# The last expert pair loaded in column halves, and the token tiles finished in another order

## The reference, cut to what matters

```python
def moe(h, ...):            # 4 groups, top-1; then top-2 of the group's 8 experts
    ...
    hg = jnp.einsum('nd,edf->nef', x, w_gate)
    hu = jnp.einsum('nd,edf->nef', x, w_up)
    act = jax.nn.silu(hg) * hu * combine[:, :, None]
    return jnp.einsum('nef,efd->nd', act, w_down)

x = x + g1 * mixers(x)      # called x1 below
x = x + g2 * moe(h2, ...)   # the outputs y_sample (4 tiles) and y_prompt (1 tile)
```

## Time and profile before

| | |
|---|---|
| median of three runs | 633.35 us |
| the profiled execution | 631.55 us, its span 629.6 us |
| TensorE, VectorE, ScalarE, GpSimd busy | 94%, 56%, 28%, 15% |
| granted TensorE clock, mean | 0.992 |
| bytes moved | 176.23 MB, mean 280 GB/s |
| chain that ended last | TensorE 67%, DMA 15%, SyncE's queue 7%, VectorE 6% |

### The profile page before, as it was taken

How to read it: one execution, slowest core, us unless ns; L and a number is a source line. 1 busy time by engine, 2 the same in 40 slices (tenths; PEclk the granted TensorE clock), 3 DMA queues, 4 the chain that set the end, 5 groups by cost and what they waited for, 6 DMA issues and landing times.

```text
span 629.6 us, 9459 instructions
## 1 busy us (share of the span) xinstructions
PE 593.3 (94%) x3309; PEld 331.4 (53%) x3310; DVE 352.3 (56%) x788; ACT 177.5 (28%) x369; POOL 94.6 (15%) x131
## 2 busy tenths in 40 slices
PE   4989999999998999999999889999999999689797
PEld 2544555555565676645555445555555555355453
DVE  2736898765664888655666873343424334313337
ACT  4203887601144787731111101101110110011110
POOL 4000011122161000000000111212122121201200
PEclk9999999999999999999999999999999999989999
DMA  8999843330029629529114959999999999999876
GB/s 318 375 370 361 318 156 138 140 133 2 0 83 280 249 92 264 238 102 398 67 68 161 382 188 392 417 419 416 420 420 410 420 417 421 419 421 416 360 280 263
DMA packets 48273, 176.23 MB, mean 280 GB/s; under 512 B 10988, under 2 KB 18168, under 8 KB 34544
## 3 DMA queue, kind: packets, MB, share of 16 engines
q1 hardware_dynamic: 36992, 154.86, 63.0%
q0 software_dynamic: 6688, 15.58, 7.1%
q10 hardware_dynamic: 4560, 5.35, 2.4%
HBM read 163.31 MB, written 21.14 MB: 293 GB/s over the span
## 4 chain that ended last, share of the span: by engine, by line
PE 67%; DMA 15%; SPq 7%; DVE 6%; issue 2%; ACT 1%; ACTq 1%; POOL 1%; DVEq 0%; POOLq 0%
PE ps L1757 16%; PE ps L1574 11%; PE ps L1773 7%; PE ps L1490 7%; PE ps L1502 6%; DMA expert_w<-exp_w_up 5%; PE ps L1612 4%; PE ps L1639 4%; DMA gate_w<-lru_wx 3%; PE ps L1621 3%; DMA w_mod_ring<-w_mod 2%; SPq L329 2%; SPq L358 2%; PE ps L1465 2%; PE ps L1725 2%
## 5 line engine op out<-in xcount | busy, mean ns | idle before, releaser
L1757 PE MATMUL ps<-expert_w,hT_mixT 128*64 128x256 f32 x1120 | 137.1, 395 | 11.9 <-DMA expert_w<-exp_w_up 11.6
L1757 PEld LDWEIGHTS ps<-expert_w,hT_mixT 128*64 128x64 f32 x1120 | 84.8, 137 | 67.6 <-issue 23.0
L1490 PE MATMUL ps<-hT_mixT,w 128*128 128x128 f32 (+1 forms) x256 | 72.6, 437 | 1.2 <-DVE hT_mixT L918 1.2
L1574 PE MATMUL ps<-w,hT_mixT 128*128 128x512 f32 x160 | 71.9, 597 | 0.0
L1773 PE MATMUL ps<-expert_w,w 128*64 128x512 f32 x280 | 65.8, 598 | 0.0
L741 ACT ACTIVATE w<-ps 128x128 f32<-128x128 f32 x36 | 10.0, 278 | 194.4 <-PE ps L1757 194.4
L1304 DVE SCALAR_TENSOR_TENSOR w<-w,ps 128x128 f32<-128x128 f32 x36 | 10.4, 288 | 88.0 <-ACT w L741 88.0
L1490 PEld LDWEIGHTS ps<-hT_mixT,w 128*128 128x128 f32 x256 | 38.9, 191 | 35.8 <-issue 32.6
L1502 PE MATMUL ps<-w_qkv,hT_mixT 128*128 128x512 f32 (+1 forms) x160 | 53.2, 488 | 0.2 <-DVE v_tok L1006 0.2
L1322 DVE TENSOR_TENSOR w<-ps,w 128x1024 f32<-128x1024 f32 x17 | 20.8, 1225 | 56.5 <-PE ps L1773 56.5
L1574 PEld LDWEIGHTS ps<-w,hT_mixT 128*128 128x128 f32 x160 | 29.1, 191 | 29.9 <-issue 29.7
(11 more groups left out here) (289 smaller groups left out, 763.6 us busy)
## 6 DMA issues: line engine op xcount, KB each, us to landing
expert_w<-exp_w_down SPq DMA_DIRECT2D x31, 1024.0 KB, 18.5
expert_w<-exp_w_gate SPq DMA_DIRECT2D x29, 1024.0 KB
expert_w<-exp_w_up SPq DMA_DIRECT2D x29, 1024.0 KB
w_mod_ring<-w_mod SPq DMA_DIRECT2D x14, 1024.0 KB, 6.5
y_rows<-zero_rows POOLq DMA_DIRECT2D x10, 512.0 KB, 9.4
expert_w<-y_rows SPq DMA_DIRECT2D x10, 512.0 KB, 8.3
recurrence<-w_mod SPq DMA_DIRECT2D x8, 512.0 KB, 9.7
w<-w_in SPq DMA_DIRECT2D x4, 1024.0 KB, 16.9
```

Of the source, the lines that this page charges most:

```text
L1490: ins = pe.matmul(ps[:, bank, 0:n], w1v[:, c, m * P:(m + 1) * P], HM[:, c, lo:lo + n], start=(c == 0), stop=(c == DC - 1))
L1574: ins = pe.matmul(ps[:, 2 * (t % 2) + half, :], HM[:, c, t * P:(t + 1) * P], w1v[:, c, half * 512:(half + 1) * 512], start=(c == 0), stop= ...
L1757: ins = pe.matmul(ps[r, 2 + k, 0:2 * P].rearrange("p (k f) -> p k f", k=2), xT[:, c, r], gate_up(i)[:, :, c, k:FF:FC], start=(c == 0), sto ...
```

## The change

Four things are changed together.

- Pair 15 is loaded by `refill_for_halves`: when the place's gate and up sums are done, eight DMAs of 512 KB (first column half of gate and up of both experts, then the second) in place of four of 1 MB. TensorE's last step waits for the first half (`halves_in`, 128), does 32 matmuls, waits for the second (`wgu_in`), does the others.
- The tiles are finished in the order 3, 4, 0, 1, 2, and `PE_SUMS` is 4, 0, 1. The y rows are read in that order.
- The three x1 reads are issued behind the y reads of tiles 3 and 4, whose x1 is in SBUF; `with_second` waits for them for tiles 0, 1 and 2 alone.
- On VectorE `with_second(3)` stands before the eviction of the last step's rows.

```diff
-PE_SUMS = (1, 2, 3)
+ORDER = (3, 4, 0, 1, 2)
+PE_SUMS = (4, 0, 1)
...
+            def refill_for_halves(q, s):
+
+                done = sp.value_load(last[0:1, q - HELD:q - HELD + 1])
+                sp.wait_ge(S["gu_mm"], done * FC)
+                for half in range(2):
+                    for j in range(2 * s, 2 * s + 2):
+                        for src, lo in ((wg_v, 0), (wu_v, EW)):
+                            sp.dma_start(ring[:, HOME[j], lo + half * EW // 2:lo + (half + 1) * EW // 2],
+                                         src[q * 2 + (j - 2 * s), :, half * EW // 2:(half + 1) * EW // 2])\
+                              .then_inc(wgu_in[s] if half else halves_in, 16)
+                sp.wait_ge(S["dn_mm"], done)
+                for j in range(2 * s, 2 * s + 2):
+                    w_down(sp, q * 2 + (j - 2 * s), j)
...
-            refill(PAIRS - 1, 0)
-            sp.wait_ge(kept_in, 16 * 4)
-            for t in range(SPILLED):
-                sp.dma_start(x1b[:, t, :], a["x1_rows"][t * P:(t + 1) * P, :]).then_inc(kept_in, 16)
+            refill_for_halves(PAIRS - 1, 0)
...
-            for t in range(NT):
+            sp.wait_ge(kept_in, 16 * 4)
+            for t in ORDER:
                 sp.dma_start(yk[:, t, :], ...).then_inc(rows_in[t], 16)
                 sp.dma_start(y0[:, t, :], ...).then_inc(y0_in[t], 16)
...
+                if t == ORDER[1]:
+                    for k in range(SPILLED):
+                        sp.dma_start(x1b[:, k, :], a["x1_rows"][k * P:(k + 1) * P, :]).then_inc(kept_in, 16)
...
             def with_second(t):
...
-                dve.wait_ge(kept_in, 16 * (4 + SPILLED))
+                if t < SPILLED:
+                    dve.wait_ge(kept_in, 16 * (4 + SPILLED))
...
+            with_second(3)
             last_y_evict(end)
+            with_first(3)
+            finish(0)
+            with_second(4)
             with_second(0)
-            with_first(0)
+            finish(1)
             with_second(1)
-            finish(0)
+            finish(2)
             with_second(2)
-            finish(1)
-            with_second(3)
-            with_second(4)
-            finish(2)
-            with_first(4)
+            with_first(2)
             finish(3)
             finish_last()
...
+                if by_halves:
+                    pe.wait_ge(halves_in, 128)
...
                 for half in range(2):
+                    if by_halves and half:
+                        pe.wait_ge(wgu_in[s], visit * 64)
```

More of the change, by code:

```diff
@@ L499, in _ @@
             sp.sem_inc(S["sp_turn"], 1)
-            for t in range(NT):
+            sp.wait_ge(kept_in, 16 * 4)
+            for t in ORDER:
                 sp.dma_start(yk[:, t, :], a["y_rows"][TOK + t * P:TOK + (t + 1) * P, :]).then_inc(rows_in[t], 16)
                 sp.dma_start(y0[:, t, :], a["y_rows"][t * P:(t + 1) * P, :]).then_inc(y0_in[t], 16)
-            for t in range(NT - 1):
-                sp.wait_ge(S["fin"], t + 1)
-                sp.dma_start(y_dst[t], yk[:, t, :]).then_inc(S["out_done"], 16)
+                if t == ORDER[1]:
+                    for k in range(SPILLED):
+                        sp.dma_start(x1b[:, k, :], a["x1_rows"][k * P:(k + 1) * P, :]).then_inc(kept_in, 16)
+            for i in range(NT - 1):
+                sp.wait_ge(S["fin"], i + 1)
+                sp.dma_start(y_dst[ORDER[i]], yk[:, ORDER[i], :]).then_inc(S["out_done"], 16)
             for half in range(2):
@@ L508, in _ @@
                 cols = slice(half * 512, (half + 1) * 512)
-                sp.dma_start(y_dst[NT - 1][:, cols], yk[:, NT - 1, cols]).then_inc(S["out_done"], 16)
+                sp.dma_start(y_dst[ORDER[-1]][:, cols], yk[:, ORDER[-1], cols]).then_inc(S["out_done"], 16)
             sp.wait_ge(S["out_done"], 16 * (NT + 2))
@@ L1343, in with_first, with finish @@
                 step(dve.tensor_tensor(yk[:, t, :], yk[:, t, :], y0[:, t, :], ALU.add))
-            def finish(t):
-                dve.wait_ge(S["tail_mm"], t + 1)
-                b = 2 * t % 8
+            def finish(i):
+                dve.wait_ge(S["tail_mm"], i + 1)
+                t, b = ORDER[i], 2 * i % 8
                 dve.tensor_tensor(yk[:, t, :], yk[:, t, :], wide[:, b * 512:b * 512 + D], ALU.add)\
@@ L1351, in finish_last @@
             def finish_last():
-                b = 2 * (NT - 1) % 8
+                t, b = ORDER[-1], 2 * (NT - 1) % 8
                 for half in range(2):
@@ L1356, in finish_last @@
                     cols = slice(half * 512, (half + 1) * 512)
-                    dve.tensor_tensor(yk[:, NT - 1, cols], yk[:, NT - 1, cols], ps[:, b + half, :], ALU.add)\
+                    dve.tensor_tensor(yk[:, t, cols], yk[:, t, cols], ps[:, b + half, :], ALU.add)\
                        .then_inc(S["fin"], 1)
@@ L1730, in act_in, with step_of @@
                 pe.transpose(ps[:, 4 + 3 * c, 0:P], act2[:, c, :], ident[:, :]).then_inc(S["aT_mm"], 1)
-            def step_of(n, s, visit, kept=False):
+            def step_of(n, s, visit, kept=False, by_halves=False):
                 def gate_up(i):
@@ L1747, in step_of @@
                     pe.wait_ge(kept_in, 16 * 4)
-                else:
+                elif not by_halves:
                     pe.wait_ge(wgu_in[s], visit * 64)
-                if s == 0 and not (isinstance(visit, int) and visit == 1):
+                if by_halves:
+                    pe.wait_ge(halves_in, 128)
+                elif s == 0 and not (isinstance(visit, int) and visit == 1):
                     pe.wait_ge(halves_in, 64)
                 for half in range(2):
+                    if by_halves and half:
+                        pe.wait_ge(wgu_in[s], visit * 64)
                     for k in range(FC):
@@ L1788, in _, with visits @@
             pe.wait_ge(S["route_ok"], 3)
-            def visits(q, s, visit, kept=False):
+            def visits(q, s, visit, kept=False, by_halves=False):
                 lo = pe.value_load(first[0:1, bass.ds(q, 1)])
@@ L1793, in visits @@
                 with pe.Fori(lo, hi) as n:
-                    step_of(n, s, visit, kept)
+                    step_of(n, s, visit, kept, by_halves)
             for s in range(HELD):
@@ L1800, in _ @@
             for q in range((BODIES - 1) * HELD, PAIRS):
-                visits(q, q % HELD, 1 + q // HELD, kept=q == KEPT // 2)
+                visits(q, q % HELD, 1 + q // HELD, kept=q == KEPT // 2, by_halves=q == PAIRS - 1)
             steps = pe.value_load(last[0:1, PAIRS - 1:PAIRS])
@@ L1806, in _ @@
             pe.wait_ge(S["xT_a"], steps + 1)
-            for t in range(NT):
-                if t >= 4:
-                    pe.wait_ge(S["fin"], t - 3)
+            for i, t in enumerate(ORDER):
+                if i >= 4:
+                    pe.wait_ge(S["fin"], i - 3)
                 if t in PE_SUMS:
@@ L1812, in _ @@
                 for half in range(2):
-                    if t == 0:
+                    if i == 0:
                         pe.wait_ge(S["y_v"], steps + 1 + half)
                     if t in PE_SUMS:
-                        pe.matmul(ps[:, 2 * t % 8 + half, :], ident[:, :], y0[:, t, half * 512:(half + 1) * 512],
+                        pe.matmul(ps[:, 2 * i % 8 + half, :], ident[:, :], y0[:, t, half * 512:(half + 1) * 512],
                                   start=True, stop=False)
-                    ins = pe.matmul(ps[:, 2 * t % 8 + half, :], chosen[:, t, :],
+                    ins = pe.matmul(ps[:, 2 * i % 8 + half, :], chosen[:, t, :],
                                     y[:, half * 512:(half + 1) * 512], start=t not in PE_SUMS, stop=True)
-                    if half or t == NT - 1:
+                    if half or i == NT - 1:
                         ins.then_inc(S["tail_mm"], 1)
```

## The result

The changed kernel takes 634.42 us (median of 20 runs, 632.44 to 637.9); the kernel before, in 20 runs beside it, 632.32 (629.74 to 634.2). The ratio is 1.0034, 95% interval 1.0019 to 1.0048: 2.1 us slower, where I had forecast 0.6 faster. The profiled execution takes 632.74 us, 1.2 over that of before, with a span of 630.7. So one part of the loss stands in this trace and another, about 0.9 us, only in the median: the profiled execution is the third fastest of the 20.

The account below looks back on a forecast made before the run. The tail was taken to be VectorE's, with the reads a little ahead. VectorE ending 0.7 us earlier, plus 0.1 for TensorE's clock, gave -0.6 us: 632.7 from the median of 633.35, range 629.5 to 634.9.

Parts of the forecast that it names:

- TensorE's earlier start: Last step's gate and up sums: start at 593.0, not 596.24, take 7.47 us and end 4.9 us earlier.
- Down weights just in time: Last step's down sums, due at 601.7: their two down transfers land at 601.0 or a little over.
- The scatter: Last scatter, from 595.41: ends at 602.3 without x1 rows on its rings; first y read at 602.4 instead of 603.09.
- First read: First y read of the tail: lands 3.4 us after issue, at 605.8, where it took 4.2 us before.
- The wait of VectorE before `with_second(0)`: VectorE in the tail: idles 3 us for the x1 reads and tile 0's y row, landing at 615.2.
- Rival D: Pair 15's loads: each half-size transfer pays 2.9 us by itself on the slowest ring, end +5 us, 638.4; chance 0.03.
- Its four matmuls for a tile take 1.72 us (the pitch from 618.28 to 620.00): TensorE in the tail: a tile's sums take 1.72 us, 3.4 at half clock, tile 0's sum then at 619.9.
- 605.8 + 12 x 1.34 = 621.9: Tail reads: thirteen at 1.34 us each after the first; the last lands 2.5 us later than the tenth did.
- I count 0.1: TensorE's idling before tile 0's first row lowers its clock: 0.1 us added to the end.
- Rival A: Tail reads cost more than they free: scatter ends 603.0, first read takes 4.2 us, +0.8 to +1.2 us, 634.3; chance 0.25.

Follow-up runs that it names:

- e1: The kernel before with only pair 15 loaded in column halves; tile order, x1 reads and VectorE's order unchanged: 633.81 us, ratio 1.0019 to before.
- e4: The changed kernel with five unused 512-column matmuls on TensorE ahead of tile 0's sum: 634.37 us, ratio 1.0035 to before.
- f3: The kernel before with only TensorE's products (placed rows) first for four tiles, first-expert rows added as they land: 634.30 us, ratio 1.0028.
- f1: The changed kernel with TensorE's products (placed rows) first for four tiles, first-expert rows added as they land: 633.61 us, ratio 1.0019 to before.
- f4: The changed kernel without the three x1 reads, VectorE adding other x1 tiles instead (a measurement, not usable): 629.79 us, ratio 0.9963 to before.
- e2: The changed kernel with the x1 reads put back behind pair 15's loads, ahead of the scatter's wait: 632.58 us, ratio 1.0001 to before.
- h1: The changed kernel with three unused 512-column matmuls on TensorE ahead of tile 0's sum: 633.01 us, ratio 1.0023 to before.
- h2: e1 with three unused 512-column matmuls on TensorE ahead of tile 1's sum: 631.22 us, ratio 0.9994 to before.

## Why the prediction was wrong

What held: *TensorE's earlier start:* right, to 0.1 us (593.02, 7.42 long). *Down weights just in time:* right (0.21 us). *The scatter:* I took 6.9 us, it took 6.91. *First read:* forecast 605.8, measured 606.0. *The wait of VectorE before `with_second(0)`:* 3.71 us, forecast 3. Rival D fell: neither half was waited for (in e1's trace the second one was, 0.58 us, not the 11.7 of D). The rule behind it, in the Trainium skill's "DMA: Bandwidth & Descriptors" (Bandwidth), that transfers be batched to 1 MiB, does not price transfers that queue behind one another on full rings; this trace shows 0 us for four more. And the fixed 2.0 us that I took from "Anatomy of one DMA" stands there for DMAs issued by GpSimd; these are SyncE's.

Two steps failed, and either one alone takes the forecast's gain away.

*The step that failed in the mechanism* is "Its four matmuls for a tile take 1.72 us (the pitch from 618.28 to 620.00)". Those two rows are successive half tiles (the second half of tile 2, the first of tile 3), not the first sums of two tiles. A tile with first-expert rows takes 0.86 us four times, 3.44 us, so tile 0's sum was ready 3.8 us behind the landing at 617.6, not 1.7, and TensorE was a second bound beside VectorE: from 617.65 two such tiles and the last one's rows make 3.44 + 3.44 + 1.72 = 8.6 us, 626.3, where I had let the reads and VectorE alone set the end. e4 shows it (1.5 us of delay there, 1.4 at the end), and f3 for the kernel before. With my own landing of tile 0's row, 616.5, its sum is ready at 616.5 + 3.8 = 620.3, and VectorE has 6.1 us behind that: an end at 626.4 in place of 625.7, by this step alone.

*The second, and in size the larger,* is "605.8 + 12 x 1.34 = 621.9": the reads' pitch was 1.46 us, and the thirteenth landed at 623.5. That accounts for 1.6 us by itself; the two bounds end within 0.4 us of one another (623.5 + 3.7 = 627.2 by the reads, 627.5 measured). The last sum ended at 627.53 for a forecast 625.7. f1, with TensorE's bound taken away, ends no earlier in its trace (25.07 us after the first y read, 24.85), and without the three reads the time falls beyond the intervals (f4, and by a hair e2). f4 prices them at 4.6 us in the medians and 2.0 in the profiled executions, which the scatter's 0.7 us never paid back. I took the pitch from ten reads beside which hardly any output moved; here 0.65 MB of outputs moved while the reads landed, which is room enough for the difference but not shown as its cause.

*The third was in the text and too small:* "I count 0.1" for TensorE's lowered clock. In the profiled execution it did not fall while TensorE had sums to do in the tail, so that trace can't show it. In h1's it did, and from the first y read to the last sum that one takes 27.45 us, 2.6 more, of which a first row that landed some 1.4 us later is a part. Over the 20 runs the mean granted clock goes from 0.993 to 0.979, and the three runs of 637.5 to 637.9 us are the three with 0.981 or less. That mean is over the whole span, so it doesn't say that the clock fell in the tail. The Trainium skill says in "TensorE: Matmul & The Clock Gate" (What's actually happening) that the number of slow matmuls varies from run to run of one kernel. These runs agree: the eight matmuls at 357 us in the routing stage, which no version changes, took 3.68 us in the trace of before and 6.16 in e1's. How the 2.1 us divide between the clock and the rest in the changed kernel is not settled: h1 gives 1.4 us with overlapping intervals, f1 0.8.

Rival A, "the reads cost more than they free", had nearly the right size (634.3) and the right sign, but not the mechanism: its condition, a first landing later than 606.5, was not met. That its time fits is luck. I had given it 0.25. The range held the measured median; the sign was wrong.

## What to carry to other kernels

Before costing a stage by its bound, count how many rows of the trace make one unit of work on each engine: two engines with work per tile and a stream of landings form three bounds, and a gain on one is lost when the next is 1 us behind. Don't move a transfer out of a stretch that hides it into the last one, where it can count at its full length. Before a trace is read for what an edit did in one stage, compare when that stage starts in both traces: here 3.2 of the 3.8 us between two executions (e1 and h2) came from ahead of the only thing in which the two kernels differ. An engine that finishes early and then stands idle may be slower after it, so an early start has to come with an order that keeps it busy to the end.

## What the runs showed that I had not expected

- Three reads of 512 KB in the tail were worth 4.6 us in the median (f4), 1.5 us each, where one is 1.28 us of data; in the profiled executions they were worth 2.0 us. The rest of the median's 4.6 us is not accounted for.
- Late in the tail the full rings moved 360 GB/s (620 to 622 us), 12% under the reads of before, with the same row length. What slowed them is open.
- With three idle matmuls, 2.6 us of useless work, e1's kernel was 2.6 us faster in the median (633.81 to 631.22). Where in the run that was gained, the two traces don't settle.
